# Winograd products in eight of the eleven chunks of each gated feed-forward

## The reference, cut to what matters

```python
def swiglu(x, w_gate, w_up, w_down):
    return (jax.nn.silu(x @ w_gate) * (x @ w_up)) @ w_down

x = x + 0.5 * swiglu(rms_norm_2(x, ffn1_norm[l]), ffn1_w_gate[l], ffn1_w_up[l], ffn1_w_down[l])
... # attention and a linear recurrence, mixed
x = x + 0.5 * swiglu(rms_norm_2(x, ffn2_norm[l]), ffn2_w_gate[l], ffn2_w_up[l], ffn2_w_down[l])
```

## Time and profile before

| what | us |
|---|---|
| median of 3 runs (3381.77 to 3383.36) | 3382.36 |
| the profiled execution, whole | 3382.04 |
| its span, first to last instruction | 3380.3 |
| PE busy | 3363.0 |
| POOL, DVE and ACT busy | 1801.0, 1695.4 and 1313.9 |

### The profile page before, as it was taken

One profiled execution on the slowest core, in us unless ns is written; L12 is line 12 of the kernel. 1 busy time (PEld: TensorE's weight loads), 2 busy tenths in 40 slices (PEclk: granted clock), 3 DMA queues, 4 the chain that ended last, 5 costly groups with the idle time before them and its releaser, 6 DMA issues.

```text
span 3380.3 us, 46752 instructions
## 1 busy us (share of the span) xinstructions
PE 3363.0 (99%) x15438; PEld 2740.0 (81%) x15438; DVE 1695.4 (50%) x2673; ACT 1313.9 (39%) x1817; POOL 1801.0 (53%) x2316
## 2 busy tenths in 40 slices
PE   9999999999999999999999999999999999999999
PEld 5888777888888887888888888888887888888887
DVE  8887785544553438614434434544358334243444
ACT  4365664222232226735633222322237545532222
POOL 6444445655555555553455555555556543465554
PEclk9999999999999999999999999999999999999999
DMA  6212552322222323331223222222223222222223
GB/s 224 86 67 69 175 168 100 114 94 99 93 100 94 99 93 101 99 125 63 69 100 102 100 93 99 94 100 93 99 93 112 88 100 75 81 95 98 99 93 112
DMA packets 94459, 343.03 MB, mean 101 GB/s; under 512 B 10609, under 2 KB 11249, under 8 KB 93954
## 3 DMA queue, kind: packets, MB, share of 16 engines
q1 hardware_dynamic: 86978, 312.11, 27.4%
q10 hardware_dynamic: 7360, 29.29, 2.7%
HBM read 335.03 MB, written 2.13 MB: 100 GB/s over the span
## 4 chain that ended last, share of the span: by engine, by line
PE 78%; issue 10%; POOL 7%; DVE 2%; DVEq 1%; ACT 1%; DMA 0%; ACTq 0%; POOLq 0%; SPq 0%
PE ps L494 24%; PE ps L496 24%; PE ps L495 24%; POOL w_lo L485 7%; PE ps L986 1%; PE ps L968 1%; PE ps L660 1%; PE ps L661 1%; PE ps L662 1%; DVE arena L2301 0%; PE ps L977 0%; DVEq L2303 0%; PE ps L626 0%; POOL xres L463 0%; DVE arena L1857 0%
## 5 line engine op out<-in xcount | busy, mean ns | idle before, releaser
L485 POOL TENSOR_TENSOR w_lo<-raw,w_hi 128x256 fp32r<-128x256 f32 x2256 | 1776.6, 818 | 1557.1 <-ACT w_hi L1074 1557.0
L1074 ACT ACTIVATE w_hi<-raw 128x1024 fp32r<-128x1024 f32 x566 | 595.9, 1055 | 1025.9 <-PE ps L496 1007.8
L494 PE MATMUL ps<-a_hi,w_lo 128*128 128x512 f32 x2208 | 873.6, 396 | 0.3 <-DVE a_lo L1803 0.3
L496 PE MATMUL ps<-a_hi,w_hi 128*128 128x512 f32 x2208 | 860.7, 390 | 0.0
L495 PE MATMUL ps<-a_lo,w_hi 128*128 128x512 f32 x2208 | 859.9, 389 | 0.0
L494 PE MATMUL ps<-b_hi,w_lo 128*128 128x512 f32 x2112 | 823.9, 390 | 4.2 <-DVE b_lo L1875 4.0
L495 PE MATMUL ps<-b_lo,w_hi 128*128 128x512 f32 x2112 | 822.5, 389 | 0.0
L496 PE MATMUL ps<-b_hi,w_hi 128*128 128x512 f32 x2112 | 822.4, 389 | 0.0
L494 PEld LDWEIGHTS ps<-a_hi,w_lo 128*128 128x128 f32 x2208 | 414.8, 188 | 100.3 <-issue 16.9
L496 PEld LDWEIGHTS ps<-a_hi,w_hi 128*128 128x128 f32 x2208 | 414.4, 188 | 87.8
L495 PEld LDWEIGHTS ps<-a_lo,w_hi 128*128 128x128 f32 x2208 | 414.9, 188 | 82.6 <-issue 0.5
(11 more groups left out here) (286 smaller groups left out, 2772.3 us busy)
## 6 DMA issues: line engine op xcount, KB each, us to landing
raw<-in_stream SPq DMA_DIRECT2D x567, 512.0 KB, 3.3
arena<-in_mod_w ACTq DMA_DIRECT2D x32, 512.0 KB, 4.2
arena<-in_mod_w SPq DMA_DIRECT2D x16, 512.0 KB, 11.5
arena<-arena ACTq DMA_DIRECT2D x16, 256.0 KB, 3.6
arena<-cum_rows ACTq DMA_DIRECT2D x2, 2048.0 KB, 8.0
xres<-in_x_t SPq DMA_DIRECT2D x4, 512.0 KB, 5.1
arena<-in_first SPq DMA_DIRECT2D x8, 256.0 KB, 11.7
xres<-in_x_t ACTq DMA_DIRECT2D x1, 2048.0 KB, 9.5
```

What stands on the lines that cost most here:

```text
L485: last = pool.tensor_tensor(w_lo[:, s, part], raw[:, s, part], w_hi[:, s, part].bitcast(F32), ALU.subtract)
L494: pe.matmul(out, lo, x_hi, start=start, stop=False)
L496: return pe.matmul(out, hi, x_hi, start=False, stop=stop)
L1074: act.activation(w_hi[:, slot, :], raw[:, slot, :], ACT.Copy).then_inc(hi_ready, 1)
```

## The change

The first three chunks of each feed-forward (`PLAIN`) stay as they are; the last eight (`FAST`) are computed in another way. There the gate product of a chunk (256 features, 1024 deep, 512 tokens) and the up product are each cut in halves in all three directions. Winograd's variant of Strassen's method makes each of them of seven products of half the size (128 features, 512 deep, 256 tokens) in place of eight.

- **PE** (`fast_product`, `fast_chunk`): a half-size product is 12 matmuls with 256 streamed tokens; a chunk has 14 of them, and then the eight down tiles as before.
- **Weight sums.** Each of the two weight matrices needs four sums of 128x512, made by DVE from the loaded units (`sums`). With them, a chunk has nine units in place of six: `g1`, `g2`, `gate_s23`, `u1`, `u2`, `up_s23`, `both_s4`, `d1`, `d2`, numbered 0 to 8. ACT rounds them (`fast_round`) and POOL makes their low parts, now in two instructions of 128x512 (`low(..., 2)`). The ring of three slots for `w_hi` and `w_lo` stays. Sum 2 of a kind ends what unit 1 or 4 waits for; sum 4 what units 2, 5 and 6 wait for.
- **Activation sums.** They are made once for each feed-forward, beside chunks 1 and 2: DVE normalises x fully (`normalise_x`), ACT rounds (`round_xn`, `round_turns`), DVE and POOL make sums and low parts (`make_turns`, `low_turns`). So the products by `rt` fall away in the fast chunks.
- **Results.** DVE combines the seven products in PSUM (`combine`, `combine_last`, 14 instructions of 256 tokens in a chunk), after ACT has copied the first product of each kind to SBUF (`copy_first`).
- **Order.** The hidden values of a chunk are made after its eight down tiles are read, then the four sums of the next chunk's up weights. The sums of the next gate weights lie between the combinations. In the last fast chunk the hidden values are made after down tiles 1 and 4 instead.
- **SP** loads six units for a chunk, each when the units made of it have their low parts.

The diff, cut to its core:

```diff
+PLAIN = 3
+FAST = FFN_CHUNKS - PLAIN
+GROUP, FAST_UNITS, FAST_TILES = 6, 9, 22
+TOK = S // 2
...
+        def fast_units(part):
+
+            g1, g2, u1, u2, d1, d2 = fast_raw(part)
+            return [g1, g2, gate_s23, u1, u2, up_s23, both_s4, d1, d2]
...
+        FAST_BANK = (0, 0, 2, 0)
+        UP_BANKS = [0, 1, 6, 7]
+        DOWN_ORDER = (2, 3, 1, 0, 1, 0, 2, 3)
...
+                with sp.Fori(1, FAST) as i:
+                    for j, unit in enumerate((2, 2, 5, 5, 7, 8)):
+                        sp.wait_ge(fast_lo, i * FAST_UNITS + (done - FAST_UNITS + unit + 1))
+                        sp.dma_start(to[j], stream[bass.ds(i * GROUP + (at + j), 1)].rearrange("o p n -> p (o n)")
+                                     ).then_inc(fast_loaded[j], 16)
...
-                    for q in range(4):
-                        part = slice(q * 2 * P, (q + 1) * 2 * P)
-                        last = pool.tensor_tensor(w_lo[:, s, part], raw[:, s, part], w_hi[:, s, part].bitcast(F32), ALU.subtract)
-                    last.then_inc(lo_ready, 1)
+            def low(to, of, hi, pieces=4):
+
+                for q in range(pieces):
+                    at = slice(q * D // pieces, (q + 1) * D // pieces)
+                    last = pool.tensor_tensor(to[:, at], of[:, at], hi[:, at].bitcast(F32), ALU.subtract)
+                return last
...
+            n = 0
+            for part in range(PARTS):
+                end = ENDS[part]
+                for stop, k in ((end - 5, 0), (end - 2, 1), (end - 1, 2), (end, 3)):
+                    low_run(n, stop)
+                    low_turns(part, k)
+                    n = stop
+                with pool.Fori(0, FAST) as i:
+                    for j, of in enumerate(fast_units(part)):
+                        s = (end + j) % RING
+                        pool.wait_ge(fast_hi, i * FAST_UNITS + (part * FAST * FAST_UNITS + j + 1))
+                        low(w_lo[:, s, :], of, w_hi[:, s, :], 2).then_inc(fast_lo, 1)
...
-                with loop(pe, FFN_CHUNKS // 2, c, units=12, tiles=24, act=4, dve=20, hid=4):
+                for chunk in range(1, PLAIN):
                     up()
-                    down(0)
-                    up()
-                    down(1)
-                down(0)
+                    down((chunk - 1) % 2)
+                c.part.n += 1
+                pe.wait_ge(turns_ready, 4 * c.part.n)
+                fast_chunk(True)
+                with loop(pe, FAST - 1, c, fast_lo=FAST_UNITS, gate_silu=2, up_read=2, down_read=8, hid=2):
+                    fast_chunk(False)
+
+                def banks_read(m):
+                    if m in (0, 2, 3):
+                        pe.wait_ge(down_read, c.down_read.at({0: -2, 2: -1, 3: 0}[m]))
+
+                down(1, banks_read)
                 c.dve.ring = 2
+
+            def fast_product(out, j, half, operand):
+
+                pe.wait_ge(fast_lo, c.fast_lo.at(j + 1))
+                s = (c.units.n + j) % RING
+                for k in range(4):
+                    w = slice(half * 4 * P + k * P, half * 4 * P + k * P + P)
+                    x_hi, x_lo = operand(k)
+                    last = mm3(out, w_hi[:, s, w], w_lo[:, s, w], x_hi, x_lo, k == 0, k == 3)
+                last.then_inc(fast_done, 1)
...
+            def fast_chunk(first):
+
+                left, right = slice(0, TOK), slice(TOK, S)
+                gate_banks = fast_banks(c.part.n - 1)
+                assert (c.dve.n + c.dve.shift) % WIDE == FAST_BANK[c.part.n - 1]
+                for banks, j in ((gate_banks, 0), (UP_BANKS, 3)):
+                    x, z, y, w = banks
...
+                    free(-3, -2)
+                    fast_product(ps[:, x, left], j, 0, x_1a)
+                    free(-2, -3)
+                    fast_product(ps[:, z, left], j, 1, x_2a)
+                    free(-1, -1)
+                    fast_product(ps[:, y, right], j + 1, 0, t_1)
+                    fast_product(ps[:, y, left], j + 1, 1, t_4)
+                    fast_product(ps[:, z, right], j + 2, 0, t_2)
+                    free(0, 0)
+                    fast_product(ps[:, w, left], j + 2, 1, t_3)
+                for half, banks in enumerate((gate_banks, UP_BANKS)):
+                    pe.wait_ge(first_copied, c.gate_silu.at(1 + half))
+                    fast_product(ps[:, banks[0], right], 6, half, x_2b)
+                pe.wait_ge(hidden_ready, c.hid.at(2))
+                for m in range(8):
...
+                    j, bank = 7 + m // 4, gate_banks[DOWN_ORDER[m]]
+                    pe.wait_ge(fast_lo, c.fast_lo.at(j + 1))
+                    s = (c.units.n + j) % RING
+                    for k in range(2):
+                        at = slice(k * 4 * P + m % 4 * P, k * 4 * P + m % 4 * P + P)
+                        last = mm3(ps[:, bank, :], w_hi[:, s, at], w_lo[:, s, at], a_hi[:, k, :], a_lo[:, k, :], k == 0, k == 1)
+                    last.then_inc(fast_done, 1)
...
+            def fast_round(j, chunk):
+
+                raw_at = {0: 0, 1: 1, 3: 2, 4: 3, 7: 4, 8: 5}
+                if j in raw_at:
+                    act.wait_ge(fast_loaded[raw_at[j]], c.fast_raw.at(16 * chunk + 16))
+                if j in (1, 2, 6):
+                    act.wait_ge(gate_summed, c.gate_sums.at(4 * chunk + {1: 2, 2: 4, 6: 4}[j]))
+                if j in (4, 5, 6):
+                    act.wait_ge(up_summed, c.up_sums.at(4 * chunk + {4: 2, 5: 4, 6: 4}[j]))
+                slot = (ENDS[c.part.n] + j) % RING
+                act.activation(w_hi[:, slot, :], fast_units(c.part.n)[j], ACT.Copy).then_inc(fast_hi, 1)
...
+            def fast_silu(m):
+
+                bank = fast_banks(c.part.n)[2 * m]
+                act.wait_ge(gate_ready, c.gate_ready.at(2 - m))
+                act.activation(sgate[:, m, :], ps[:, bank, :], ACT.Silu).then_inc(gate_silu, 1)
...
+            def copy_first(bank, to):
+                act.activation(to, ps[:, bank, 0:TOK], ACT.Copy).then_inc(first_copied, 1)
+
+            def fast_chunk(last):
+
+                for j in range(3, FAST_UNITS):
+                    act.wait_ge(fast_done, c.fast.at(2 * (j - 2)))
+                    fast_round(j, 0)
+                    if j == 4:
+                        act.wait_ge(hidden_ready, c.hid.at(0))
+                        copy_first(fast_banks(c.part.n)[0], gate_m1)
+                    if j == 6:
+                        fast_silu(1)
+                        copy_first(UP_BANKS[0], up_m1)
+                fast_silu(0)
+                for j, tiles in enumerate((14, 18, 22)):
+                    act.wait_ge(fast_done, c.fast.at(tiles))
+                    if not last:
+                        fast_round(j, 1)
+                    elif j < LEAD:
...
+            def normalise_x(g, k):
+
+                for i in range(2):
+                    last = dve.scalar_tensor_tensor(x_turns[k][:, i * S:i * S + S], xres[:, 4 * i + k, :], par(PAR2, g, 4 * i + k), rt,
+                                                    ALU.mult, ALU.mult)
+                last.then_inc(xn_ready, 1)
+
+            def make_turns(k):
+
+                x_1a, x_1b, x_2a, x_2b = (x_turns[k][:, i * TOK:i * TOK + TOK] for i in range(4))
+                dve.wait_ge(xn_rounded, 4 * c.part.n + k + 1)
+                dve.tensor_tensor(q11_lo[:, k, :], x_1a, q11_hi[:, k, :].bitcast(F32), ALU.subtract)
+                dve.tensor_tensor(a_lo[:, 4 + k, :], x_turns[k][:, S:2 * S], a_hi[:, 4 + k, :].bitcast(F32), ALU.subtract)
+                dve.drain()
+                dve.tensor_tensor(x_1a, x_1b, x_1a, ALU.subtract)
+                dve.drain()
+                dve.tensor_tensor(x_1b, x_2b, x_1b, ALU.subtract)
+                dve.drain()
+                dve.tensor_tensor(x_2b, x_2b, x_1a, ALU.subtract)
+                dve.drain()
...
+                raws = fast_raw(c.part.n)
+                one, two = raws[0:2] if gate else raws[2:4]
+                s23, s4 = (gate_s23, both_s4[:, 0:S]) if gate else (up_s23, both_s4[:, S:2 * S])
+                summed = gate_summed if gate else up_summed
+                for n in range(first, end):
+                    dve.drain()
+                    if n == 0:
+                        for j in (0, 1) if gate else (2, 3):
+                            dve.wait_ge(fast_loaded[j], c.fast_raw.at(16 * chunk + 16))
+                        if chunk:
+                            dve.wait_ge(fast_lo, c.fast_lo.at(3 if gate else 6))
+                        dve.tensor_tensor(s23[:, S:2 * S], one[:, 0:S], two[:, 0:S], ALU.subtract).then_inc(summed, 1)
+                    if n == 1:
+                        dve.tensor_tensor(two[:, 0:S], two[:, 0:S], two[:, S:2 * S], ALU.add).then_inc(summed, 1)
+                    if n == 2:
+                        dve.tensor_tensor(s23[:, 0:S], two[:, 0:S], one[:, 0:S], ALU.subtract).then_inc(summed, 1)
+                    if n == 3:
+                        if chunk:
+                            dve.wait_ge(fast_lo, c.fast_lo.at(7))
```

(126 more changed lines are left out.)

209 lines of the change are left out of this document (181 added, 28 removed).

## The result

The changed kernel is slower: 3431.0 us median of four runs (3428.76 to 3434.05) against 3382.53 (3381.77 to 3383.36), a ratio of 1.0144 with a 95% interval of 1.0126 to 1.0161. That is above the forecast of 3390 to 3420 and near the upper end of the range, 3434. The profiled execution is 3428.76 us, its span 3427.0 against 3380.3.

A forecast was written before the change was run, and what follows sets the result against it. PE's own stream was taken to bound the feed-forwards. 3382.0 - 51 (PE's work) + 78 (waits) = 3409 us, less 5 for rounding against the change, gave 3404; forecast 3390 to 3420, 8-in-10 range 3360 to 3434.

The forecast's parts named there:

- the schedule: Hand-made timeline of PE, DVE, POOL and ACT in a steady fast chunk: waits of 2.3 us, chunk 33.3, not 31.05.
- wait at unit 4: Steady fast chunk: PE free at 11.6 us after E, unit 4 ready at 12.7, a wait of 1.1.
- two hidden values of 2.46 each: DVE after the last down tile of a fast chunk: two hidden values, 2.46 us each, done by 5.8 after E.
- rival C: Slower still: POOL loses more beside DVE, or a unit stays at 2.8 us; 3434 us, chance 0.16.
- POOL's loss: POOL's low parts: each 512-wide DVE instruction with two SBUF inputs beside them takes 0.48 us from POOL.
- the up sums 1.31 each: DVE's up sums 0 and 1 behind the hidden values: 1.23 us beside POOL plus 0.08 drain each, until 8.4.
- PE's own time: A fast chunk on PE without waits: 31.05 us, 1.6 less a chunk, -51 us over 32 chunks.
- four last fast chunks: Eighth fast chunk of each feed-forward: a hidden value between down tiles 1 and 2; waits of 2.7 us.
- plain chunks: Unchanged chunks with added DVE work: late down tiles cost 0 to 3 us, 1.5 taken for each feed-forward.
- B: No contention with long pieces: sums cost 0.69 us, POOL a flat 2.5; 3337 us, chance 0.08.
- A: Faster: same chain, shorter links, sums 1.07 us, POOL's loss 0.4, restart 0.15; 3365 us, chance 0.19.
- D: A draw: waits equal the gain, 1.6 to 1.9 us a chunk; 3376 to 3389 us, chance 0.14.

The follow-up runs named there:

- run 3: Changed kernel with DVE's weight sums shrunk to one column in seven of eight fast chunks, all waits and signals kept: 3365.12 us, ratio 0.9949.
- run 8: Changed kernel with POOL making only the first 512 columns of each low part in the fast chunks, in one instruction: 3333.91 us.
- run 4: Changed kernel with the product of silu and up written back to PSUM, where rounding and low part read it: 3382.84 us, ratio 1.0001.
- run 5: Changed kernel with the next up sums made after reads of down tiles 4 to 7, ahead of the hidden values: 3343.66 us, ratio 0.9887.
- run 6: Changed kernel with both edits, hidden values kept in PSUM and up sums made during the down tiles: 3341.64 us, ratio 0.9881.
- run 1: Changed kernel with low parts of the fast chunks' units in four instructions of 128x256 in place of two: 3444.07 us, ratio 1.0182.
- run 7: Changed kernel with hidden values in PSUM, up sums during the down tiles, and low parts in four instructions: 3376.2 us, runs from 3359.28 to 3387.51.

## Why the prediction was right in sign and place, and wrong in size

**Right.** The direction, and where it comes from: a wait for `w_lo` at unit 4, behind the hidden values and up sums; the loads are no part of it. Counting from E, the end of the last down tile (3207.33 here), the schedule stands against the trace so:

| step | forecast | measured |
|---|---|---|
| two hidden values done | 5.8 | 7.8 |
| unit 3 has its low part | 8.4 | 7.3 |
| up sum 1 done | 8.4 | 9.6 |
| unit 4 rounded, ACT starts | 8.5 | 9.6 |
| POOL ends unit 4 | 12.4 | 13.5 |
| PE wanted unit 4 | 11.6 | 11.3 |
| wait at unit 4 | 1.1 | 2.2 |
| units 5 and 6, waits together | 1.1 | 0.5 |

**The step that failed** is the price of DVE's instructions beside POOL, "two hidden values of 2.46 each". Those rows have 128x256 pieces beside them, and I carried 0.69, 0.53 and 1.07 over to 128x512 pieces. In run 3 DVE stands until POOL's piece is over, and the pieces are now twice as long. A value is 3.4 there: the rounding 1.23 or 0.76, the low part 1.63 or 1.51. That is 2.0 us on the chain. The same page of rows held the hint: L1810 and L1803 reach 1.23, so 1.07 was no ceiling. I did name "a long piece leaves fewer gaps", in rival C, but as POOL's loss; the runs show that DVE bears it. POOL's loss, at most 0.5 a piece, was sized about right (0.48). The second error went the other way: I gave the up sums 1.31 each for contention, but POOL has nothing to do by then, for it waits for those very sums, and they take 0.79 with their gap. So 2.0 late became 1.2 late. A third was small: PE restarts 0.05 us after POOL's last piece and then loses 0.1, where I had 0.27.

**PE's own time** is 30.79 a chunk and not 31.05, as a half-size step takes 0.118 in a long run of them (168 in a row in run 8) and not 0.120. The change brought 1.87 a chunk, 60 us, where I had 51. It did not help: PE only came to unit 4 earlier.

**The clock** was not in the sum. Before, the trace has one stretch of 3.4 us at 1.2 GHz; after, twelve, nine of them in steady chunks and two in last ones. These eleven come behind waits of 2.2 us, of which there are 28, so not every such wait brings one. None is left in the fast chunks of runs 3 to 6 and 8, whose waits are shorter; the few in the fast chunks of runs 1 and 7 come behind waits of 2.1 us for a bank, in first fast chunks. The cause was not tested by itself.

**The account.** The four feed-forwards grew by 11.0, 13.4, 10.9 and 11.2 us, from PE's starts in both traces: 46.6, all of the span's 46.7. Forecast and measured, in us for all four:

| part | forecast | measured |
|---|---|---|
| 32 fast chunks of PE alone, against 32.65 | -51 | -60 |
| 24 steady chunks, beyond PE alone | 2.1 each, 50 | 3.0 each, 72 |
| lower clock in nine of them | 0 | 7 |
| four first fast chunks, beyond PE alone | 6.4 | 4.9 |
| four last fast chunks (34.3, 35.8, 34.4, 35.8) | 10.8 | 17.0 |
| plain chunks (88.7, 88.2, 88.7, 88.2 for 87.1) | 6.0 | 5.5 |
| sum | 22 | 46 |

The last chunks carry a wait for the bank of down tile 2 (1.1) and the 2.2 of unit 4, and two of them a stretch of low clock. The plain chunks came out as chosen: one wait of 1.07 in each feed-forward behind DVE, and 0.5 more in two of them.

**The rivals.** B (no contention) is refuted by L2636's two levels. C had nearly the right number (3434 against 3431), but by luck, for its mechanism is wrong: POOL loses no more than 0.5 a piece, two pieces alone take 2.55 and not 2.8, and run 5 shows POOL's loss to be harmless when the order is right. A got its cheap sums and its short restart, but not its time (3365), since the hidden values ahead of them were dearer; run 4 shortens these and reaches 3383, run 5 takes them off the chain and reaches 3344. D wanted waits of 1.6 to 1.9 us a chunk, and they were 3.0.

## What to carry to other kernels

A duration read beside one shape of POOL instruction is no price beside another: where a change alters the pieces of one engine, the instructions of the others that run beside it have to be priced anew, with a range that goes well above the dearest row: here DVE waits for the piece beside it, and the pieces had doubled. Before calling a change bound by an engine's throughput, look whether that engine was idle just before the late unit: then it is the order ahead of it that costs, and moving one group of instructions (here the up sums into the gaps between down tiles, 87 us) does more than shortening them. An intermediate value that one engine reads several times can be kept in PSUM to stay clear of POOL.
